# RWKV inverse levels and read-out products: one product for both heads of a pair instead of one for each head

## The reference, cut to what matters

```python
def step(s, inp):
    r_t, w_t, k_t, v_t, kk_t, a_t = inp
    sa = jnp.einsum('bhvk,bhk->bhv', s, kk_t)
    s = (s * w_t[:, :, None, :] - sa[..., None] * (kk_t * a_t)[:, :, None, :]
         + v_t[..., None] * k_t[:, :, None, :])
    return s, (jnp.einsum('bhvk,bhk->bhv', s, r_t) if emit else None)
```

## Time and profile before

| | us |
|---|---|
| median of three runs | 1650.59 |
| lowest and highest | 1650.26, 1653.68 |
| the profiled execution | 1652.26 |
| its span | 1650.2 |

### The profile page before, as it was taken

One profiled execution on the slowest core, in us unless ns is written; L12 is line 12 of the kernel. 1 busy time (PEld: TensorE's weight loads), 2 busy tenths in 40 slices (PEclk: granted clock), 3 DMA queues, 4 the chain that ended last, 5 costly groups with the idle time before them and its releaser, 6 DMA issues.

```text
span 1650.2 us, 33271 instructions
## 1 busy us (share of the span) xinstructions
PE 1586.6 (96%) x14140; PEld 1321.7 (80%) x14140; DVE 944.0 (57%) x1497; ACT 799.6 (48%) x1315; POOL 312.5 (19%) x251
## 2 busy tenths in 40 slices
PE   8999999988899999999999999999998889999998
PEld 6788767767678887888888886987877779899987
DVE  5364555565465569655554225655776277677764
ACT  4322456473354266443443225525766365566653
POOL 0160234323110000112222000312352220012210
PEclk9999999999999999999999999999999899999999
DMA  9753334223852352322226343843413285645453
GB/s 332 198 166 102 102 103 160 75 99 102 266 192 91 113 191 77 102 91 88 95 71 111 106 123 126 261 128 115 143 56 130 55 281 179 215 165 181 164 189 134
DMA packets 213889, 234.42 MB, mean 142 GB/s; under 512 B 5936, under 2 KB 194736, under 8 KB 213744
## 3 DMA queue, kind: packets, MB, share of 16 engines
q1 hardware_dynamic: 194208, 191.14, 35.3%
q0 software_dynamic: 14928, 34.87, 7.9%
q10 hardware_dynamic: 4608, 6.29, 1.1%
HBM read 216.55 MB, written 15.73 MB: 141 GB/s over the span
## 4 chain that ended last, share of the span: by engine, by line
PE 70%; DVE 4%; issue 3%; ACT 3%; DMA 0%; POOL 0%; ACTq 0%; DVEq 0%; POOLq 0%
PE ps L2337 15%; PE ps L2338 15%; PE ps L2339 15%; PE ps L2633 1%; PE ps L2645 1%; PE ps L2428 1%; PE ps L2794 1%; PE ps L2793 1%; PE ps L2792 1%; PE ps L2685 1%; PE ps L2402 1%; PE ps L2404 1%; PE ps L2403 1%; PE ps L2362 1%; PE ps L2363 1%
## 5 line engine op out<-in xcount | busy, mean ns | idle before, releaser
L1065 ACT ACTIVATE whi<-ring 128x1024 fp32r<-128x1024 f32 (+1 forms) x262 | 274.5, 1052 | 481.6 <-PE ps L2339 424.6
L1610 DVE TENSOR_TENSOR wlo<-ring,whi 128x1024 fp32r<-128x1024 f32 (+1 forms) x262 | 327.5, 1254 | 175.5 <-ACT whi L1065 174.8
L2337 PE MATMUL ps<-H,whi 128*128 128x256 f32 (+1 forms) x640 | 215.4, 337 | 1.8 <-DVE wlo L1610 1.8
L2339 PE MATMUL ps<-H,wlo 128*128 128x256 f32 (+1 forms) x640 | 214.9, 336 | 0.0
L2338 PE MATMUL ps<-H,whi 128*128 128x256 f32 (+1 forms) x640 | 214.9, 336 | 0.0
L2337 PE MATMUL ps<-HR,whi 128*128 128x512 f32 (+1 forms) x568 | 202.1, 356 | 0.5 <-DVE wlo L1610 0.3
L2339 PE MATMUL ps<-HR,wlo 128*128 128x512 f32 (+1 forms) x568 | 198.3, 349 | 0.0
L2338 PE MATMUL ps<-HR,whi 128*128 128x512 f32 (+1 forms) x568 | 198.2, 349 | 0.0
L2337 PEld LDWEIGHTS ps<-H,whi 128*128 128x128 f32 x640 | 122.3, 191 | 14.2 <-issue 1.9
L2338 PEld LDWEIGHTS ps<-H,whi 128*128 128x128 f32 x640 | 122.2, 191 | 12.2
L2339 PEld LDWEIGHTS ps<-H,wlo 128*128 128x128 f32 x640 | 122.3, 191 | 12.0
(11 more groups left out here) (397 smaller groups left out, 3279.9 us busy)
## 6 DMA issues: line engine op xcount, KB each, us to landing
ring<-in_ffn_up SPq DMA_DIRECT2D x44, 1024.0 KB, 5.0
ring<-in_w_gate SPq DMA_DIRECT2D x32, 1024.0 KB, 5.9
ring<-in_ada_w SPq DMA_DIRECT2D x32, 1024.0 KB, 5.3
ring<-in_w_in SPq DMA_DIRECT2D x24, 1024.0 KB, 7.6
ring<-in_ffn_down SPq DMA_DIRECT2D x10, 1024.0 KB, 5.0
ring<-in_ffn_down SPq DMA_DIRECT2D x18, 512.0 KB, 3.8
ada<-in_ada_w SPq DMA_DIRECT2D x8, 1024.0 KB, 11.7
WB<-in_w_branch POOLq DMA_DIRECT2D x8, 1024.0 KB, 6.5
```

The lines of the kernel that those rows point to most:

```text
L1065: act.activation(whi[HALF_SLOT[m]][:, 0:kn, :], ring_half(raw, half, kn), ACT.Copy).then_inc(hi_done, 1)
L1610: dve.tensor_tensor(wlo[HALF_SLOT[m]][:, 0:kn, :], ring_half(raw, half, kn), whi[HALF_SLOT[m]][:, 0:kn, :].bitcast(F32), ALU.subtract).the ...
L2337: pe.matmul(o[:, c0:c1], hi[:, i, :], part(0, k), start=(k == 0), stop=False)
L2339: last = pe.matmul(o[:, c0:c1], lo[:, i, :], part(0, k), start=False, stop=(k == kn - 1))
```

## The change

`sx`, `sy` and `y23` take both heads of a pair in one product.

- `sx`: weights are `LM1` of both heads (64 rows, 128 columns) and the moving side is the even blocks of both heads of `TN` (64 columns instead of 32). The result is 128 by 64 for each chunk, and the half of it in which the heads differ is not wanted. The masks `m2` to `m32` are twice as wide and hold zeros for the other head, so `XS` is twice as wide and keeps each head's own block.
- `sy`: weights are `TT` of both heads (128 rows, 64 columns) and the moving side is the masked `XS` (64 columns). The zeros keep the heads apart.
- `y23`: weights are `v` and `nu` of both heads (64 rows, 128 columns), the moving side `LM2` and `LM1` of both heads (128 columns). VectorE adds each head's own block in an operation of its own: two on 64 partitions in place of one on 128.
- `LM1`, `LM2`, `nu` are laid out with both heads side by side. ScalarE's copy of `U0` takes the sign, so `nu` is a copy and a subtraction. The table of constants is 160 columns wider.

```diff
-            for b, x, y in corners():
-                last = pe.matmul(o[side(y), x, CH2 * b:CH2 * b + CH2].rearrange("k (g n) -> k g n", n=z),
-                                 LM1[side(x), 2 * p + y, b, 0:CH], even_blocks(TN[side(x), p, b, y, :], z),
+            for b, x in chunks:
+                both = TN[side(x), p, b, :, :].rearrange("p y n -> p (y n)")
+                last = pe.matmul(o[:, x, CH * b:CH * b + CH].rearrange("k (g n) -> k g n", n=z),
+                                 LM1[side(x), p, b, 0, :, :].rearrange("k y n -> k (y n)"), even_blocks(both, z),
                                  start=True, stop=True)
...
-            for b, x, y in corners():
-                last = pe.matmul(o[side(x), y, CH2 * b:CH2 * b + CH2], TT[side(y), p, b, x, :],
-                                 XS[side(y), p, x, b, :], start=True, stop=True)
+            for b, x in chunks:
+                last = pe.matmul(o[side(x), 0, CH * b:CH * b + CH], TT[:, p, b, x, :],
+                                 XS[:, p, x, b, :], start=True, stop=True)
...
-            for y in range(2):
-                h = 2 * p + y
-                pe.matmul(o[side(y), x, dst], tokm["v"][side(x), b, HD * h:HD * h + HD],
-                          LM2[side(x), h, b, CH:2 * CH], start=True, stop=False)
-            for y in range(2):
-                h = 2 * p + y
-                last = pe.matmul(o[side(y), x, dst], nu[side(x), b, y, HD * p:HD * p + HD],
-                                 LM1[side(x), h, b, CH:2 * CH], start=False, stop=True)
+            dst = o[:, x, P * at_b:P * at_b + P]
+            heads = lambda v: v.rearrange("k y n -> k (y n)")
+            pe.matmul(dst, tokm["v"][side(x), b, P * p:P * p + P], heads(LM2[side(x), p, b, 1, :, :]),
+                      start=True, stop=False)
+            last = pe.matmul(dst, heads(nu[side(x), b, p, :, :]), heads(LM1[side(x), p, b, 1, :, :]),
+                             start=False, stop=True)
...
-            s = filled(dve, ("y23", l, d, p))[:, :, 0:256].rearrange("p x (b n) -> p x b n", b=NB)[:, :, 2 * l:, :]
-            v = YB[:, 6 + p, c0:T].rearrange("p (b x n) -> p x b n", x=2, n=CH)
-            dve.tensor_tensor(v, v, s, ALU.add).then_inc(frees(("y23", l, d, p)), 1)
+            s = filled(dve, ("y23", l, d, p)).rearrange("p x (b y n) -> p x b y n", b=NB, y=2)[:, :, 2 * l:, :, :]
+            for y in range(2):
+                v = YB[side(y), 6 + p, c0:T].rearrange("p (b x n) -> p x b n", x=2, n=CH)
+                o = s[side(y), :, :, y, :]
+                ins = dve.tensor_tensor(v, v, o, ALU.add)
+            ins.then_inc(frees(("y23", l, d, p)), 1)
...
-        put(f"m{z}", ((s // z) % 2 == 1) & (even // z == s // z - 1))
+        own = ((s // z) % 2 == 1) & (even // z == s // z - 1)
+        put(f"m{z}", np.concatenate([own & (p[:, None] // CH == y) for y in range(2)], 1))
...
-            dve.scalar_tensor_tensor(nu[q, b, :, :], s[q, :, 0:P], -1.0, drop, ALU.mult, ALU.subtract)\
+            taken = s[q, :, 0:P].rearrange("p y (a n) -> p y a n", a=2)
+            dve.tensor_tensor(own, drop, taken, ALU.subtract)\
```

More of the change, by code:

```diff
@@ L541, in build @@
         qroot = [rs, rt, YB[:, 4, :]]
-        nu = at("nu", 164, [NB, 2, P])
+        nu = at("nu", 164, [NB, 2, 2, HD])
         state = at("state", 112, [NCH, 2, HD])
@@ L549, in build @@
         TN = at("TN", 84, [2, NB, 2, CH])
-        XS = at("XS", 88, [2, 2, NB, CH2])
+        XS = at("XS", 88, [2, 2, NB, 2 * CH2])
         XV = at("XV", 92, [2, 2, NB, CH])
-        LM1 = at("LM1", 96, [HEADS, NB, 2 * CH])
-        LM2 = at("LM2", 104, [HEADS, NB, 2 * CH])
+        LM1 = at("LM1", 96, [2, NB, 2, 2, CH])
+        LM2 = at("LM2", 104, [2, NB, 2, 2, CH])
         U0 = at("U0", 84, [NB, 2, 2, HD])
@@ L705, in even_blocks @@
         def even_blocks(v, z):
-            if len(v.shape) == 2:
-                return v.rearrange("p (g two n) -> p g two n", two=2, n=z)[:, :, 0, :]
-            return v.rearrange("p b y (g two n) -> p b y g two n", two=2, n=z)[:, :, :, :, 0, :]
+            return v.rearrange("p (g two n) -> p g two n", two=2, n=z)[:, :, 0, :]
         def done_at(name):
@@ L1968, in _ @@
                         for p in range(2):
[L1969 to L1970 removed]
+                            s = filled(dve, ("sx", l, d, z, p))[:, :, 0:NB * CH].rearrange("p x (b n) -> p x b n", b=NB)
+                            dve.tensor_tensor(XS[:, p, :, :, :], s, own_head(f"m{z}"), ALU.mult)\
                                .then_inc(frees(("sx", l, d, z, p)), 1)
@@ L1980, in _ @@
                         for p in range(2):
-                            s = filled(dve, ("sy", l, d, z, p))[:, :, 0:NB * CH2]                                .rearrange("p y (b g n) -> p b y g n", b=NB, n=z)
-                            t = even_blocks(TN[:, p, :, :, :], z)
+                            s = filled(dve, ("sy", l, d, z, p))[:, 0, 0:NB * CH].rearrange("p (g n) -> p g n", n=z)
+                            t = even_blocks(TN[:, p, :, :, :].rearrange("p b y n -> p (b y n)"), z)
                             if n:
@@ L2005, in _ @@
                         q, b = side(c % 2), c // 2
-                        drop = U0[q, b, :, :, :].rearrange("p y a n -> p y (a n)")
+                        drop = U0[q, b, :, :, :]
+                        own = nu[q, b, :, :, :].rearrange("p a y n -> p y a n")
                         if c == 0:
-                            dve.tensor_scalar(nu[q, b, :, :], drop, -1.0, None, ALU.mult).then_inc(nu_done, 1)
+                            dve.tensor_copy(own, drop).then_inc(nu_done, 1)
                         else:
                             s = filled(dve, ("cu", l, d, c))
-                            dve.scalar_tensor_tensor(nu[q, b, :, :], s[q, :, 0:P], -1.0, drop, ALU.mult, ALU.subtract)\
+                            taken = s[q, :, 0:P].rearrange("p y (a n) -> p y a n", a=2)
+                            dve.tensor_tensor(own, drop, taken, ALU.subtract)\
                                .then_inc(frees(("cu", l, d, c)), 1)
@@ L2597, in token_major @@
                         done(last)
+                    chunks = [(c // 2, c % 2) for c in range(NCH)]
                     def corners():
@@ L2676, in _ @@
                                     h = 2 * p + y
-                                    last = pe.matmul(o[side(y), x, CH * b:CH * b + CH], LM2[side(x), h, b, 0:CH],
+                                    last = pe.matmul(o[side(y), x, CH * b:CH * b + CH], LM2[side(x), p, b, 0, y, :],
                                                      tokm["v"][side(x), b, HD * h:HD * h + HD], start=True, stop=True)
@@ L2736, in _ @@
                                 last = pe.matmul(o[side(y), HD * p:HD * p + HD], tokm["b"][side(x), b, hs],
-                                                 nu[side(x), b, y, HD * p:HD * p + HD], start=False, stop=(p == 1),
+                                                 nu[side(x), b, p, y, :], start=False, stop=(p == 1),
                                                  skip_group_check=True)
```

24 lines of the change are left out of this document (12 added, 12 removed).

## The result

| | us |
|---|---|
| before, median of six runs | 1652.66 (1650.26 to 1654.57) |
| after, median of six runs | 1668.26 (1664.33 to 1675.94) |
| ratio after to before | 1.0099, 95% interval 1.0078 to 1.0121 |
| the profiled execution of after, its span | 1664.33, 1662.5 |

What follows compares the result with a forecast made beforehand. TensorE's program in its order was taken as the bound. 15.6 + 4.1 + 1.6 - 14.1 - 4.2 = +3.0 on 1652.26 gave 1655.3 us, or 1655.0 in terms of the runs (0.27% slower), range 1643 to 1664.

Steps and rivals of the forecast that it cites:

- sx: `sx` in the levels of four passes: rounds of 0.11 us by loading 128 columns, +16.2 us, 15.6 after hiding.
- Rival 1: `sx` goes at the rate of its stream, a round stays 0.058 us: 1639 us, faster; chance 10%.
- sy: `sy` in the levels: 16 rounds before and after, 0 us, bounds -0.05 and +0.8 a level.
- change of tile shape: TensorE in front of `sy` (ten places) and at `y23` (six): 0.1 us each, +1.6 us.
- y23: Read-outs of the passes: `y23` takes 3.5 us in place of 1.9 in layer 0; +4.1 us in sum.
- rival 4: Products of 64x128 don't overlap, in `sx` or between chunks in `y23`: +5 to +17, 1660 to 1672 us; chance 6%.
- The waits for instructions: TensorE's "issue" waits in levels, `u0` and `y23` shrink with fewer instructions: -14.1 us, bounds 0 and -16.1.
- Rival 2: The "issue" waits don't come from the number of instructions and stay: 1673 us, 1664 if half goes; chance 10%.
- The wider masks and additions of VectorE: VectorE in the passes: wider `XS`, masks and two more `y23` additions a pass are covered, 0 us.
- The clock: Three half-clock stretches behind instruction waits in the passes go: -4.2 us, bounds +2 and -6.
- The tail: Behind the last read-out: `y23`'s extra VectorE additions lie under the 1.10 us wait for `WL`, 0 us.

Runs made afterwards that it cites:

- pair of candidates: Changed kernel, `sx` per head, `w_branch` transfer issued at `y1`: with `y23` for both heads 1647.68 us (0.9969), with `y23` per head too 1653.34 (1.0017).
- sx_back: Changed kernel with `sx` alone made for each head again, `sy` and `y23` for both: 1653.34 us, ratio 1.0007 to before.
- y23_back: Changed kernel with `y23` made for each head again, all else changed: 1669.39 us, ratio 1.0092 to before.
- early transfer: Changed kernel with a layer's first `w_branch` transfer issued when `y1`, not `y23`, of its second pass is done: 1666.22 us, ratio 1.0096 to before.

## Why the forecast was wrong, step by step

*`sx`: right, a little small.* Forecast 0.81 a level from a step of 0.11 between loads of 128 columns; measured 0.87, 17.4 in place of 16.2 over 20 levels, and 18.2 in the medians with `sx` undone. Rival 1, a round at the rate of the stream, is excluded by the run with twice the columns. The Trainium skill (TensorE: Matmul & The Clock Gate, LDWEIGHTS) has this rule, a load's time by its columns, and the runs bear it out: 0.112 a round against its 0.107. The forecast's "the trace agrees" was weaker than it sounds, since it solved its two rows with one step for both shapes; the loads themselves show it, 0.11 apart at L2436 and, in pairs, in the changed `sx`.

*`sy`: right.* 0, by the level of 4.92 us with `sx` back. The change of tile shape in front of it costs its 0.11 a level, but the wait at the level's end takes it in: 1.0 of the +1.6 was not due.

*`y23`: right in length* (3.6 against 3.5), and rival 4, that products of 64x128 don't overlap, did not come. That it would be the cheaper form all the same, because its waits weigh more, is in the sum (4.1 against waits of 2.50 and 2.79 and more). The pair of candidates bears it out in the medians; the waits seen there explain only part of it.

*The waits for instructions: right in kind, the size too large.* Forecast −14.1 of 16.1; in the profiles they fell from 19.5, 16.5 and 16.2 to 6.6, 5.5 and 6.3, a mean of 11.3. Nearly all of that (13.3 to 2.8) is in the waits inside a job, of which the forecast spoke. It had its sum from the profile with the most of them. Packets of the instruction queue in the passes of layer 1 fell from 26 to 20 (1205 to 1345). Rival 2 fell. The wider masks and additions of VectorE cost nothing, as said.

*The clock: the size near, the reasoning only half right.* The forecast took 5.2 for what three slow stretches of one profile cost (of five in it) and gave back 1.0 for one that falls slow elsewhere. It took the stretches as tied to the waits that went. The half clock in the passes was 20.8, 24.1 and 36.7 us in the profiles before (mean 27.2) and is 6.8, 37.5 and 17.0 after (20.4). Taken at half its length that is 3.4 us won in the mean against 4.2 forecast, but the nearness is luck: up to the chunks it fell from a mean of 16.6 to 3.4, in the chunks and read-outs it rose from 10.6 to 17.0, and two profiles of one kernel lie up to 16 us (before) and 31 us (after) apart. That the first profile's passes grew by 4.1, near the sum's +3.0, is luck too: taking any profile after with any before gives −1.3 to +16.1. The mean is +8.0.

*The tail: this step failed.* The forecast priced the longer `y23` behind the last read-out at 0. It looked at VectorE's additions alone, behind which "stands `WL`, which VectorE waits 1.10 us for in layer 1 anyway", took that wait as cover and did not follow it on. VectorE waits there for ScalarE's `WH`, and `WH` needs the transfer of `w_branch`, which is issued behind `y23`, the very job that the change makes 0.9 us longer there. The real cover was the 0.8 us by which that transfer landed before ScalarE came to it. The tail grew by 8.1 us in the mean of the profiles; the grouping above gives some 6 of them to this wait and what comes with it. That `y23` is behind it and not `sx` is shown by `sx_back` (wait 4.23, landing 8.2 us after the issue) against `y23_back` (landing after 6.0) and the early transfer (wait 1.57, landing after 6.3). A lateness of about 1 us alone would not make 2.8 of waiting; the other part is that the transfer itself takes 8.3 us in place of 5.9, and 7.8 or more in all seven profiles in which a transfer of `w_gate` is issued within about 1 us of it. What slows it there was not tried.

Of the 15.6 us the forecast had 3.0, the tail is 8.1, the passes are 5.0 above the sum in the mean of the profiles, and 1.2 are won between. With the terms as the runs gave them (`sx` +16.8, tile shapes +0.6, the waits −11.3, the clock −3.4) and `y23` as forecast, the sum for the passes is +6.8 against the +8.0 of the profiles. This is an estimate, since profiles of one kernel scatter by 7 to 10 us in the passes; by it the waits (2.8) are the larger part of the 5.0, then `sx` (1.2) and the clock (0.8).

## What to carry to other kernels

For small products count the columns of the weights, not the multiplications: two heads side by side in the columns of the weights double the load and so the time of the product, two heads one above the other in the rows (as `sy`) cost nothing here and halve the instructions. For each job that a change makes longer, list what its completion releases on every queue, transfers on GpSimd above all, and follow a wait back to its transfer before calling it cover. Where slow stretches of the clock enter a sum, take more than one profile of the kernel before: here two of them differ by up to 16 us in how long they are.

## What the runs showed of the hardware

- A stretch at the half clock can be as long as 30.7 us in a phase of short dependent products (pass (0,1), chunks, TensorE busy all the while by its rows), and costs 11.1 us over the chunks and the read-out of that pass, somewhat over a third of its length.
- A wait of TensorE of 3.8 to 5.2 us in a stream of products that were dense until then came with a stretch at the half clock, which begins within it or up to 0.9 us behind its end, in seven profiles of seven; with the wait at 1.5 to 1.6 in the same place it was three of nine.
- A wait called "issue" is of two kinds: in the middle of a job it went with the number of instructions (a mean of 13.3 us to 2.8); in front of a whole `sx` it stayed to within 0.2 us, and the level after it has the same 0.64 under the name of `TN`.
- Two products of 64x128 weights side by side take 0.112 us, with 64 or 128 moving columns; two of 128x64 take 0.058, as four of 64x64 do.
- The 1 MB of `w_branch` issued 1.7 us or more ahead of the next 1 MB of `w_gate` landed in 5.9 to 7.2 us, issued 0.5 ahead of it or 1.0 behind it in 7.8 to 9.2 (nine and seven profiles).
